# Stream 2 of a two-block transformer kernel: the group shares spread by stacked fp32r matmuls, four gates of the last source computed ahead of its branch products

## What is computed

```
outs, lses = [], []
for gi, (window, dil) in enumerate(ATT_GROUPS):                  # 3 groups, 8 heads of 64
    o_g, l_g = dilated_window_attention(q_b[:, :, gi], k_b[:, :, gi], v_b[:, :, gi], slopes[gi], dil, window // (2 * dil))
    outs.append(o_g); lses.append(l_g)
wts = jax.nn.softmax(jnp.stack(lses), axis=0)                     # a share per group, token and head
o_b = jnp.einsum('gbsh,gbshe->bshe', wts, jnp.stack(outs))
y_b = o_b.reshape(b, s, ATT_OUT_WIDTH).astype(x.dtype) @ w_attn_out
mixed = jax.nn.sigmoid(gate_a) * y_a + jax.nn.sigmoid(gate_b) * y_b    # y_a = o_a @ w_dn_out
x = x + mixed @ w_o
```

## Time and profile before

| | us |
|---|---|
| median of three runs | 3118.15 (3116.43 to 3118.99) |
| the profiled execution, its own time | 3108.3 |
| its span in the profile | 3106.5 |
| PE busy | 2924.3 (94%) |
| DVE busy | 2114.3 (68%) |
| ACT busy | 1586.4 (51%) |
| mean granted clock of PE | 0.969 of full |

### The profile page before, as it was taken

One profiled execution on the slowest core, in us unless ns is written; L12 is line 12 of the kernel. 1 busy time (PEld: TensorE's weight loads), 2 busy tenths in 40 slices (PEclk: granted clock), 3 DMA queues, 4 the chain that ended last, 5 costly groups with the idle time before them and its releaser, 6 DMA issues. The chain is left out here.

```text
span 3106.5 us, 46231 instructions
## 1 busy us (share of the span) xinstructions
PE 2924.3 (94%) x18534; PEld 2342.4 (75%) x18534; DVE 2114.3 (68%) x2176; ACT 1586.4 (51%) x1765; POOL 280.5 (9%) x225
## 2 busy tenths in 40 slices
PE   5999999789999999999999959899899999899999
PEld 4777777468887888887888847688778877678877
DVE  6578644569999999989999975466464454366642
ACT  3556433347777777777777734222354542333321
POOL 0110100001111111111111000344000000000000
PEclk9999999789999999999999979899899998999999
DMA  6332343269999999999999972000221222323321
GB/s 247 128 106 89 110 134 109 109 253 367 374 375 363 372 378 375 373 369 371 373 371 369 370 277 68 16 4 4 92 67 59 75 70 81 109 82 94 95 82 68
DMA packets 217372, 607.95 MB, mean 196 GB/s; under 512 B 10784, under 2 KB 118304, under 8 KB 183424
## 3 DMA queue, kind: packets, MB, share of 16 engines
q1 hardware_dynamic: 202480, 554.87, 48.3%
q0 software_dynamic: 14592, 50.36, 4.7%
q10 hardware_dynamic: 144, 0.53, 0.0%
HBM read 582.62 MB, written 23.10 MB: 195 GB/s over the span
## 5 line engine op out<-in xcount | busy, mean ns | idle before, releaser
L2491 DVE TENSOR_TENSOR weight_ring_part<-weight_ring,weight_ring_part 128x2048 fp32r<-128x2048 f32 x380 | 852.9, 2286 | 104.3 <-ACT weight_ring_part L2430 103.5
L2430 ACT ACTIVATE weight_ring_part<-weight_ring 128x2048 fp32r<-128x2048 f32 x380 | 713.7, 1915 | 255.7 <-PE ps L193 137.5
L193 PE MATMUL ps<-weight_ring_part 128*128 128x512 f32 x1456 | 576.8, 396 | 0.0
L189 PE MATMUL ps<-weight_ring_part,gathered_hi 128*128 128x512 f32 x1024 | 408.6, 399 | 0.0
L293 DVE TENSOR_TENSOR weight_ring_part<-weight_ring,weight_ring_part 128x2048 fp32r<-128x2048 f32 x111 | 253.2, 2281 | 225.5 <-ACT weight_ring_part L290 223.6
L193 PE MATMUL ps<-weight_ring_part,gathered_hi 128*128 128x512 f32 x1024 | 405.2, 396 | 0.0
L192 PE MATMUL ps<-weight_ring_part,gathered_lo 128*128 128x512 f32 x1024 | 405.1, 396 | 0.0
L189 PE MATMUL ps<-h1T_hi,weight_ring_part 128*128 128x512 f32 x872 | 357.5, 410 | 3.1 <-DVE weight_ring_part L293 1.7
L192 PE MATMUL ps<-h1T_hi,weight_ring_part 128*128 128x512 f32 x872 | 346.0, 397 | 0.0
L193 PEld LDWEIGHTS ps<-weight_ring_part 128*128 128x128 f32 x1456 | 275.3, 189 | 68.9
L290 ACT ACTIVATE weight_ring_part<-weight_ring 128x2048 fp32r<-128x2048 f32 x111 | 211.1, 1902 | 135.8 <-PE ps L193 104.0
(11 more groups left out here) (491 smaller groups left out, 4382.9 us busy)
## 6 DMA issues: line engine op xcount, KB each, us to landing
weight_ring<-in_w SPq DMA_DIRECT2D x190, 2048.0 KB, 8.8
weight_ring<-in_w_in SPq DMA_DIRECT2D x58, 1024.0 KB, 5.2
weight_ring<-in_w_ffn_up SPq DMA_DIRECT2D x44, 512.0 KB, 4.9
weight_ring<-in_w_ffn_down SPq DMA_DIRECT2D x11, 1024.0 KB, 4.8
mod_tile<-in_w_ada POOLq DMA_DIRECT2D x36, 256.0 KB, 3.1
weight_ring<-in_w_ada SPq DMA_DIRECT2D x8, 1024.0 KB, 12.9
gate_rows<-in_w_ada POOLq DMA_DIRECT2D x28, 256.0 KB, 3.1
weight_ring<-in_w_branch SPq DMA_DIRECT2D x6, 1024.0 KB, 5.2
```

Of the source, the lines that this page charges most:

```text
L189: first = nc.tensor.matmul(out, x[0], y[0], start=start, stop=False)
L193: return nc.tensor.matmul(out, x[0], y[1], start=False, stop=stop)
L2430: nc.scalar.activation(hi_half(h), full_half(h), ACT.Copy).then_inc(w_rounded, 1)
L2491: nc.vector.tensor_tensor(lo_half(h), full_half(h), hi_half(h), ALU.subtract).then_inc(w_split, 1)
```

## The change

It has four parts.

1. The shares are spread by fp32r matmuls. ACT rounds the shares to their high part on partitions 0 to 7 of a tile `parts` (`w_round`), DVE puts the low part on partitions 32 to 39 (`w_split`). The selector stands twice, at the same partitions. One matmul over 40 partitions, cleared to zero beforehand where nothing stands, adds both parts. Clearing and the selector's fp32r copies are a new ACT job `w_clear`, after the last use of that room by the attention's normalisation. SP loads the selector twice.
2. In source 1, first half, the four gate elements stand ahead of the four branch elements; their tanh goes to room of its own (the attention's v rows, free once the last unit's values are read). The weights' units in the ring are in that order too.
3. `w_mul` and `w_sum` have rank 4 in place of 0, below the split of a weight unit (rank 3).
4. Some lengths in the planner are other ones (`logs` 0.6 for 2.0, `w_spread` 0.3 for 0.9).

```diff
@@ ring
-                ring.add(tall(a[w][0], 0)[:, :, 512 * j:512 * j + 512], BC, 512)
-                ring.add_pair(wide(w_in2, c0 + 512 * j), DK, 512, by_rows=False)
+                if w == "w_dn_out_2" or j:
+                    ring.add(tall(a[w][0], 0)[:, :, 512 * j:512 * j + 512], BC, 512)
+                    ring.add_pair(wide(w_in2, c0 + 512 * j), DK, 512, by_rows=False)
+                else:
+                    ring.add_pair(wide(w_in2, c0 + 512 * j), DK, 512, by_rows=False)
+                    ring.add(tall(a[w][0], 0)[:, :, 512 * j:512 * j + 512], BC, 512)
@@ lay_out
-                    needs += [("gate", gates[i - 2]) if i >= 2 else None, gate_after if i == 0 else None]
+                    needs += [("weigh", N - 1) if x["early"] else ("gate", gates[i - 2]) if i >= 2 else None, gate_after if i == 0 else None]
...
+                job(("w_clear",), "act", 4.5, 4, ("spread", len(batches) - 1, len(batches[-1]["keys"]) - 1))
+                job(("w_round",), "act", 2.0, 0, ("weights",), ("w_clear",))
+                job(("w_split",), "dve", 1.9, 0, ("w_round",))
                 for n in range(3 * BC):
-                    job(("w_spread", n), "pe", 0.9, 1, ("weights",), ("w_mul", n - 4) if n >= 4 else None, ("w_spread", n - 1) if n else None)
-                    job(("w_mul", n), "dve", 0.85, 0, ("w_spread", n), ("w_mul", n - 1) if n else None)
-                job(("w_sum",), "dve", 5.0, 0, ("w_mul", 3 * BC - 1))
+                    job(("w_spread", n), "pe", 0.3, 1, ("w_split",), ("w_mul", n - 4) if n >= 4 else None, ("w_spread", n - 1) if n else None)
+                    job(("w_mul", n), "dve", 0.85, 4, ("w_spread", n), ("w_mul", n - 1) if n else None)
+                job(("w_sum",), "dve", 5.0, 4, ("w_mul", 3 * BC - 1))
@@ stream, TensorE
-                            pe.wait_ge(weights_ready, 1)
-                            pe.wait_ge(selector_loaded, 16)
+                            pe.wait_ge(shares_split, 1)
...
-                        nc.tensor.matmul(ps[:, 3 + n % 4, :], lse_of["selector"][:, c, :], lse_of["turned"][:, g, :], start=True, stop=True)\
+                        nc.tensor.matmul(ps[:, 3 + n % 4, :], lse_of["selector_parts"][:, P * c:P * c + P], lse_of["parts"][:, g, :], start=True, stop=True)\
@@ stream, ScalarE
+                    def clear_parts():
+                        act.wait_ge(spread_ready, len(spread_at))
+                        nothing = const[0:40, 0:T]
+                        nc.scalar.activation(lse_of["parts"], nothing.unsqueeze(1).to_broadcast([40, 3, T]), ACT.Copy, scale=0.0)
+                        nc.scalar.activation(lse_of["selector_parts"], nothing, ACT.Copy, scale=0.0)
+                        act.drain()
+                        act.wait_ge(selector_loaded, 32)
+                        for at in (0, 32):
+                            nc.scalar.activation(lse_of["selector_parts"][at:at + 8], lse_of["selector"][at:at + 8], ACT.Copy)
+                        act.drain()
...
+                    def round_weights():
+                        act.wait_ge(weights_ready, 1)
+                        nc.scalar.activation(lse_of["parts"][0:8], lse_of["turned"], ACT.Copy).then_inc(shares_rounded, 1)
@@ stream, VectorE
+                    def split_weights():
+                        dve.wait_ge(shares_rounded, 1)
+                        nc.vector.tensor_tensor(lse_of["parts"][32:40], lse_of["turned"], lse_of["parts"][0:8], ALU.subtract).then_inc(shares_split, 1)
@@ merge_elements
+                    early = (n, half) in gates_first
+                    products = [dict(kind="branch", unit=unit + 2 * early, part=m, ends=int(m == 3), source=n) for m in range(4)]
+                    gates = [dict(kind="gate", unit=unit + (not early) + m // 2, part=m % 2, ends=m % 2, source=n, row=4 * half + m, early=early) for m in range(4)]
+                    elements += gates + products if early else products + gates
@@ build
-        merge_elements(elements, 2)
+        merge_elements(elements, 2, gates_first=[(1, 0)])
```

More of the change, by code:

```diff
@@ L1130, in copied, with gate_room @@
                     eng.wait_ge(bank_free[e % 2], e // 2 + 1)
+                def gate_room(e):
+                    return merge["early"][:, elements[e]["row"], :] if elements[e]["early"] else merge["gate"][:, gate_at[e] % 2, :]
                 @block.sync
@@ L1134, in _ @@
                     if lse_of is not None:
-                        sp.dma_start(lse_of["selector"], a["selector"].rearrange("h (c n) -> h c n", c=BC)).then_inc(selector_loaded, 16)
+                        for at in (0, 32):
+                            sp.dma_start(lse_of["selector"][at:at + 8], a["selector"]).then_inc(selector_loaded, 16)
                     if side is not None:
@@ L1366, in out @@
                                     act.wait_ge(of_name[name], count)
-                            if gate_at[e] >= 2:
+                            if x["early"]:
+                                act.wait_ge(values_read, N)
+                            elif gate_at[e] >= 2:
                                 act.wait_ge(merged, gate_at[e] - 1)
-                            nc.scalar.activation(merge["gate"][:, gate_at[e] % 2, :], bank, ACT.Tanh, scale=0.5).then_inc(bank_free[e % 2], 1)
+                            nc.scalar.activation(gate_room(e), bank, ACT.Tanh, scale=0.5).then_inc(bank_free[e % 2], 1)
                     def turn_v(e):
@@ L1476, in _ @@
                             exp_lse()
+                        elif kind == "w_clear":
+                            clear_parts()
+                        elif kind == "w_round":
+                            round_weights()
                 @block.vector
@@ L1584, in gate @@
                             dve.drain()
-                        last = nc.vector.scalar_tensor_tensor(dst, merge["gate"][:, i % 2, :], 1.0, merge["branch"][:, i % 4, :], ALU.add, ALU.mult)
+                        last = nc.vector.scalar_tensor_tensor(dst, gate_room(e), 1.0, merge["branch"][:, i % 4, :], ALU.add, ALU.mult)
                         last.then_inc(merged, 1)
@@ L1676, in _ @@
                             make_weights()
+                        elif kind == "w_split":
+                            split_weights()
                         elif kind == "w_mul":
@@ L1680, in _, with merge_elements @@
                             sum_groups()
-        def merge_elements(elements, sources):
+        def merge_elements(elements, sources, gates_first=()):
             unit = max([e["unit"] for e in elements], default=-1) + 1
@@ L1689, in merge_elements @@
                 for half in range(2):
-                    elements += [dict(kind="branch", unit=unit, part=m, ends=int(m == 3), source=n) for m in range(4)]
-                    elements += [dict(kind="gate", unit=unit + 1 + m // 2, part=m % 2, ends=m % 2, source=n, row=4 * half + m) for m in range(4)]
+                    early = (n, half) in gates_first
+                    products = [dict(kind="branch", unit=unit + 2 * early, part=m, ends=int(m == 3), source=n) for m in range(4)]
+                    gates = [dict(kind="gate", unit=unit + (not early) + m // 2, part=m % 2, ends=m % 2, source=n, row=4 * half + m, early=early) for m in range(4)]
+                    elements += gates + products if early else products + gates
                     unit += 3
@@ L3330, in build @@
         lse_m = late_room[0:8, 3 * T:4 * T]
-        selector = late_room[0:8, 4 * T:5 * T].rearrange("h (c n) -> h c n", c=BC)
+        selector = late_room[0:40, 4 * T:5 * T]
+        parts_room = arena_part[0:40, 0:2048]
         p_turned2 = late_room[:, 0:1024]
@@ L3392, in build @@
                merge=dict(sources=[(dn_out[:, :, :], half_x(x_part[:, :, :], 0), dn_out_part[:, :, :]), (o_bT, hi_b, o_g_part[:, 0])],
-                          out=chan(xn_flat, 0, DK), branch=half_x(x_tok[:, :, :], 1), room_free=[], gate_free=[], gate=arena[:, 6656:7680].rearrange("p (a b) -> p a b", a=2), gated=arena[:, 7680:8192], after=[[], [("weights_read", 13)]]),
-               side=side, lse_of=dict(sums=stats2[:, 1, :], lse=lse, turned=lse_t, most=lse_m, selector=selector, out=o_g))
+                          out=chan(xn_flat, 0, DK), branch=half_x(x_tok[:, :, :], 1), early=v_room, room_free=[], gate_free=[], gate=arena[:, 6656:7680].rearrange("p (a b) -> p a b", a=2), gated=arena[:, 7680:8192], after=[[], [("weights_read", 13)]]),
+               side=side, lse_of=dict(sums=stats2[:, 1, :], lse=lse, turned=lse_t, most=lse_m, selector=selector, out=o_g,
+                           parts=parts_room[:, 0:3 * T].rearrange("h (g t) -> h g t", g=3), selector_parts=parts_room[:, 3 * T:4 * T]))
         project_out((chan(xn_flat, 0, DK), h1T_hi, as_chunks(xn_part[:, :, :])), None, load_x=x_mid)
```

9 lines of the change are left out of this document (5 added, 4 removed).

## The result

| | before | after |
|---|---|---|
| median, us | 3117.29 of 4 runs (3115.12 to 3118.99) | 3098.35 of 4 runs (3098.07 to 3103.99) |
| profiled execution, its own time | 3108.3 | 3098.07 |
| its span | 3106.5 | 3096.2 |
| PE busy | 2924.3 | 2911.8 |
| mean granted clock | 0.969 | 0.972 |

The ratio is 0.9947, with an interval of 0.9935 to 0.996: 12.5 to 20.3 us off 3117. The kernel is faster, by 0.5%.

A forecast was written before the change was run, and what follows sets the result against it. PE was taken as the bound nearly everywhere, through its work and its lowered clock. Spreading's 20.8 us today less 5.9 after gave 14.9 off the median 3118.15, so 3103.2 us; range 3099 to 3108.5, chance of faster 0.88.

The forecast's parts named there:

- Nothing waits, the clock does: Around the 8-partition spreads PE is busy without a gap but at 1.2 GHz; spreading costs 20.8 us, 14.9 come off.
- The stretch: Elements 50 and 51 with their twelve spreads on PE: 11.15 us of steps plus 5.9 of spreads after the change.
- The 0.39 us a piece: Cost on PE of going into and out of each group of consecutive spreads; eight groups, 3.12 us.
- The times behind the stretch: After elements 50 and 51: w_sum, splits and source 1's branches, with 3.5 and 11.7 us of room for PE.
- Edits at nothing: w_clear (about 3.3 us, in ACT's idle time), w_round, w_split and the second selector load cost nothing on the path.
- Gates ahead: Source 1's gates before its branches cover its rounding and split; the old order would idle PE 9 to 10 us.
- The clock falls at the same moment: Rival, chance 0.07: PE's clock drops there whatever matmuls stand there; only 4.6 us off, 3113.5.
- Lasting fall: Rival, chance 0.03: stacked matmuls pull PE's clock down and keep it down; slower, 3140 if until the first branch.
- DVE did not become what PE waits for: Rival, chance 0.05: the 2.29 us split among the w_mul makes PE wait for DVE; 3104 to 3106.5.
- I take the difference off the median: Last step of the sum: 14.9 us subtracted from the median 3118.15 of the runs shown, giving 3103.2.

The follow-up runs named there:

- second profile of before: The kernel before, unedited, profiled and timed again: 3114.0 us against 3116.83 for the kernel before, ratio 0.999 (0.9979 to 1.0002).
- second comparison: The changed kernel, unedited, timed again in more rounds beside the kernel before: 3096.76 us against 3117.58, ratio 0.9942 (0.9925 to 0.9959).

## Why the prediction was right, and where it was off

- **Nothing waits, the clock does.** Right. Of the 14.9 us (31.94 to 17.05), 10.5 go with 128 partitions in float32 (31.94 to 21.44): about 9.7 of clock and 0.8 of partition change. The other 4.4 are the float32 passes less the pieces' price, 12 x (0.86 - 0.232) - 8 x 0.39, with 0.86 for one of them from (21.44 - 11.15) / 12.
- **The stretch.** Predicted 17.05 us; measured 17.05, twice. The 0.39 us a piece, taken from a 36-partition row, was measured at 0.39; it is the change of partition count, which the prediction had only read off, not explained. So the agreement to 0.1 us rests on a neighbour's row, not on a worked-out cost.
- **The times behind the stretch**, from the start of element 50: w_sum ends at 21.8 predicted and 21.8 measured (2584.90 - 2563.11), the split for gates 54 and 55 at 24.8 and 24.9, that of source 1 at 27.7 and 27.5, its branches start at 39.4 and 39.3.
- **Edits at nothing.** w_clear 3.3 predicted, 3.35 measured, covered; w_split's room 1.8 and 1.9. PE never waited for a bank: w_mul 1 ended at 2567.11, and the spread that needs it stood at 2569.32.
- **Gates ahead.** PE was to stand 9 to 10 us without them: it stood 9.0. What the prediction left out is that such a wait costs 2.4 us of clock behind it (1.43 us of wait in the kernel with float32 on 128 partitions did not: its clock stayed at 1.00). The ranks, for which it named no price of their own, are worth 8.2 us in the trace.
- **Rivals.** "The clock falls at the same moment": fell with the float32 matmuls on 128 partitions (1.00 throughout) and with the second profile of before, where the fall moved with the spreads. The Trainium skill's page "TensorE: Matmul & The Clock Gate", in "Part 1: The HAM clock gate", ties the lower clock to an idle engine: the wait of 5.54 us agrees with it, but by it alone the busy PE of the earlier trace rows should have kept its clock, and it didn't. "Lasting fall": not here; in the kernel with eight times the matmuls the clock stayed down for 20 us. DVE did not become what PE waits for.
- **The time.** 3103.2 predicted, 3098.35 measured: 4.85 below, and 0.65 below the range's lower end. By the ratio, 0.9947 of the 3118.15 that the prediction started from is 3101.6, inside it. The step that was off is the last one, "I take the difference off the median", with one microsecond for the scatter of that median. Three runs within 2.6 us hid a scatter of 17 (3107.01 to 3124.34 over all runs of before), and the second comparison too says about 18 off with 15 in the stretch. Both intervals hold 14.9 (0.9952). Since medians of the kernel before lay between 3114.0 and 3117.6, that term of the range should have been some 4 us to each side; the mechanism's own terms were right to 0.1.

## What to carry to other kernels

Read the granted clock beside the busy time: a PE busy in every microsecond ran at half speed for 20 us around matmuls of 8 partitions. A small product between full ones was cheapest padded with zeros to 128 partitions, 0.39 to 0.40 us less for each piece, and it counted where PE was busy without a gap, though DMA read 0.96. When work of PE is taken away, look at what it hid: without the gates ahead or without the ranks, waits give back 8 to 12 of the 15 us.

## What was not expected of the hardware

- The granted clock went to the 1.2 GHz level with PE busy without a gap, on float32 matmuls of 8 partitions (0.51 for 20.4 us) and on a run of 32 fp32r ones of 40 (0.50 for 20 us). It did not on float32 ones of 128, nor on pieces of eight and sixteen fp32r ones of 40 with product steps between (0.99 to 1.00).
- After a wait of 5.54 us PE resumed at the lower level and was back at the higher one 4.9 us later; 2.5 us of work were lost to it, and 2.4 us after a wait of 9.0 us.
- Going from 128 partitions to 8, 36 or 40 and back costs 0.38 to 0.40 us, spread over the matmul ahead, the light ones and the one behind.
